# One decode step of a hybrid trunk on one core: dense panels in quarters across nine decode turns, attention pieces first on PE

## What is computed

```python
def mixer_inputs(h, w_in, b_f, w_g2, b_g):
    z = h @ w_in                    # 2048 -> 6168: FoX q, k, v; GLA q, k, v, r; two narrow gate groups
    ...
def fox_sample(q, k_new, v_new, logf_new, k_past, v_past, logf_past):   # decode: 8 requests, 8 heads
    s_past = jnp.einsum('bthd,bshd->bhts', q, k_past, preferred_element_type=jnp.float32) * scale
    ...
    p = jax.nn.softmax(jnp.concatenate([s_past, s_new], axis=-1), axis=-1).astype(v_new.dtype)
    return (jnp.einsum('bhts,bshd->bthd', p[..., :P], v_past)
            + jnp.einsum('bhts,bshd->bthd', p[..., P:], v_new))
def gla_prompt(q, k, v, g): ...     # 4 GLA heads over 256 tokens, in chunks of 64
def gla_chunk(S0, q, k, v, g): ...  # also one step for each decode request's own state
def memory_kv(mem, g_mem, w_k, w_v): ...   # 256 memory tokens
# x += [FoX heads, GLA heads] @ w_out ; x += cross_attn(...) ; x += swiglu(...) ; final rmsnorm
```

## Time and profile before

| | us |
|---|---|
| runs of the kernel | 1799.93, 1797.80, 1799.86 (median 1799.86) |
| the profiled execution | 1794.59 |
| its span, first to last instruction | 1792.9 |
| start to the eighth panel's end | 82.4 |
| turns 0 to 8 and the norm of the heads | 704.6 (82.4 to 787) |
| `out` panels to the end | 1005.9 |

### The profile page before, as it was taken

One profiled execution on the slowest core, in us unless ns is written; L12 is line 12 of the kernel. 1 busy time (PEld: TensorE's weight loads), 2 busy tenths in 40 slices (PEclk: granted clock), 3 DMA queues, 4 the chain that ended last, 5 costly groups with the idle time before them and its releaser, 6 DMA issues.

```text
span 1792.9 us, 33586 instructions
## 1 busy us (share of the span) xinstructions
PE 1571.9 (88%) x12269; PEld 1449.2 (81%) x12269; DVE 1057.7 (59%) x3260; ACT 633.0 (35%) x758; POOL 232.2 (13%) x332
## 2 busy tenths in 40 slices
PE   5999989784965667869967999999999999999997
PEld 5999868673843444569946999999999999999997
DVE  4557868577686886476664555555344555554444
ACT  3342322213242231344344433333333333333443
POOL 3000122222112222213211100000000000000221
PEclk9999989886977757789978999999999999999998
DMA  7456889987869688564541454454455555544553
GB/s 285 174 177 254 334 348 357 374 338 276 309 203 333 224 273 313 195 260 172 181 130 59 142 188 177 176 186 165 148 182 200 182 179 186 184 172 141 181 177 129
DMA packets 85736, 388.24 MB, mean 217 GB/s; under 512 B 9080, under 2 KB 19072, under 8 KB 63760
## 3 DMA queue, kind: packets, MB, share of 16 engines
q1 hardware_dynamic: 36048, 230.90, 36.2%
q0 software_dynamic: 39376, 143.15, 22.0%
q10 hardware_dynamic: 10224, 13.12, 2.1%
HBM read 377.03 MB, written 10.10 MB: 216 GB/s over the span
## 4 chain that ended last, share of the span: by engine, by line
PE 64%; DVE 13%; DMA 4%; issue 3%; ACT 2%; POOLq 0%; POOL 0%; DVEq 0%; ACTq 0%
PE bank L1443 19%; PE bank L1444 18%; PE bank L1445 18%; DVE page L958 4%; DVE wlo L881 2%; DMA page<-vc_dram 2%; PE bank L1562 2%; DMA page<-kc_dram 1%; ACT whi L503 1%; PE bank L1653 1%; DMA g_s<-s_dram 1%; DVE g_dd L1124 0%; DVE g_d L1162 0%; DVE g_s L1132 0%; PE bank L1760 0%
## 5 line engine op out<-in xcount | busy, mean ns | idle before, releaser
L1443 PE MATMUL bank<-hh,whi 128*128 128x264 f32 (+1 forms) x2560 | 739.0, 289 | 13.2 <-DVE wlo L881 8.7
L1444 PE MATMUL bank<-hl,whi 128*128 128x264 f32 (+1 forms) x2560 | 731.0, 286 | 0.0
L1445 PE MATMUL bank<-hh,wlo 128*128 128x264 f32 (+1 forms) x2560 | 730.3, 285 | 0.0
L503 ACT ACTIVATE whi<-raw 128x2048 fp32r<-128x2048 f32 (+1 forms) x232 | 410.2, 1768 | 815.4 <-PE bank L1445 810.4
L881 DVE TENSOR_TENSOR wlo<-raw,whi 128x2048 fp32r<-128x2048 f32 (+1 forms) x232 | 489.1, 2108 | 333.0 <-ACT whi L503 332.7
L1443 PEld LDWEIGHTS bank<-hh,whi 128*128 128x128 f32 x2560 | 488.9, 191 | 25.8 <-issue 20.0
L1444 PEld LDWEIGHTS bank<-hl,whi 128*128 128x128 f32 x2560 | 489.2, 191 | 1.0 <-issue 0.7
L1445 PEld LDWEIGHTS bank<-hh,wlo 128*128 128x128 f32 x2560 | 486.4, 190 | 0.0
L958 DVE CUSTOM_DVE_ANT_0 page<-page,qb 128x128 f32<-128x128 f32 x1024 | 225.4, 287 | 67.6 <-DMA page<-kc_dram 50.1
L1443 PE MATMUL bank<-f_hi,whi 128*128 128x264 f32 x704 | 201.9, 287 | 7.5 <-DVE f_lo L1415 7.5
L1445 PE MATMUL bank<-f_hi,wlo 128*128 128x264 f32 x704 | 201.4, 286 | 0.0
(11 more groups left out here) (273 smaller groups left out, 1266.7 us busy)
## 6 DMA issues: line engine op xcount, KB each, us to landing
raw<-p_gu_dram SPq DMA_DIRECT2D x88, 1024.0 KB, 4.8
page<-kc_dram POOLq DMA_DIRECT2D x128, 512.0 KB, 5.8
page<-vc_dram POOLq DMA_DIRECT2D x128, 512.0 KB, 5.9
raw<-p_dn_dram SPq DMA_DIRECT2D x64, 704.0 KB, 4.0
raw<-p_fox_dram SPq DMA_DIRECT2D x24, 1024.0 KB, 5.0
raw<-p_gla_dram SPq DMA_DIRECT2D x24, 1024.0 KB, 7.1
raw<-p_out_dram SPq DMA_DIRECT2D x16, 1024.0 KB, 4.8
raw<-p_mem_dram SPq DMA_DIRECT2D x8, 1024.0 KB, 8.1
```

The lines of the kernel that those rows point to most:

```text
L503: act.activation(whi[:, kk % 2, 0:blocks * P], raw[:, kk, 0:blocks * P], ACT.Copy).then_inc(S("w_hi"), 1)
L1443: mm(out, blk(whi, k % 2, b), rh, start=start, stop=False)
L1444: mm(out, blk(whi, k % 2, b), rl, start=False, stop=False)
L1445: return mm(out, blk(wlo, k, b), rh, start=False, stop=stop)
```

## The change

The FoX and GLA panels become one list of 48 (`p_in`), with columns in a new order: FoX q, GLA q, k, v, then FoX k and v by head, then GLA r. Eight panels run at the start. The other 40 and the 8 memory panels are cut into quarters of four blocks (12 matmuls) and are dealt over nine turns of 16 parts by the table `QUARTERS`: 8, 8, 3, 3, 5, 5, 6, 4 and 6 panels. A part of a turn has one K page on DVE. In every part PE first does its attention pieces and then the part's quarters. Two more tables deal the V pages (`VALUES`) and the heads (`HEAD_AT`). States are in turns 2 and 3, the GLA heads in turns 2 to 5, the FoX heads in turns 6 and 7, the memory's norm in turn 7, the norm of the GLA heads in turn 8. Head buffers move out of the ring to free parts of `z` and elsewhere; copies of q and v for the heads go, since q is scaled when it leaves the bank and PE reads `z`. The new token's share of the softmax is worked once for all requests in turn 8. POOL fetches the pages in the order in which the parts use them (`page_places`). At the start, panel 0 goes ahead of the sums of the norm, and its weights are loaded after a quarter of x. The `out` panels read their rows from `zr`. All loops over turns are written out. From the `out` panels on the order is as before.

```diff
-MIX = [("k", j) for j in range(8)] + [x for j in range(8) for x in (("v", 2 * j), ("v", 2 * j + 1), ("k", 8 + j))]
+IN, TURNS = 48, 9
+QUARTERS = ([2] * 16,) * 2 + ([1, 1, 1, 0] * 4,) * 2 + ([1, 1, 1, 2] * 4,) * 2 + (
+    [2, 1] * 8, [2] * 4 + [0] * 6 + [1, 1, 1, 1, 2, 2], [2, 1] * 8)
+VALUES = ([0] * 4 + [1, 1, 2] * 4,) * 8 + ([0] * 4 + [2] * 8 + [0] * 4,)
+HEAD_AT = (1, 3, 7, 9, 13, 18, 19, 24)
+def quarters(t, j):
+    first = 32 + sum(sum(q) for q in QUARTERS[:t]) + sum(QUARTERS[t][:j])
+    return [(n // 4, n % 4) for n in range(first, first + QUARTERS[t][j])]
...
+def page_places():
+    where = {}
+    for t in range(TURNS):
+        for j in range(16):
+            if t < ND:
+                where["k", t, j] = len(where)
+            for v in values(t, j) if t else ():
+                where["v", t - 1, v] = len(where)
...
+            first_x(0)
+            weights(0)
+            first_x(1)
+            first_x(2)
...
+            def panel_step(p):
+                act.wait_ge(S("mm_done"), p + 1)
+                panel_cast(p + 2)
...
+            for g in range(16 * TURNS):
+                t, j = g // 16, g % 16
...
+                for p in finished(g - 1):
+                    panel_evac(p)
...
+                elif t < ND:
+                    k_page(t, j)
+                for p in finished(g - 1):
+                    panel_split(p + 2)
...
+                if t >= 1:
+                    softmax_turn(t, j)
...
+            def quarter(p, q):
+                n = T if p < IN else MEM
+                if q == 0:
+                    pe.wait_ge(S("w_split"), p + 1)
+                    pe.wait_ge(S(f"acc{p % 2}_free"), p // 2 + 1)
+                for b in range(4 * q, 4 * q + 4):
...
+                    last = three(bank[p % 2][:, 0:n], p % 4, b, hh[:, b, 0:n], hl[:, b, 0:n], b == 0, b == C - 1)
+                if q == 3:
+                    last.then_inc(S("mm_done"), 1)
...
+            for g in range(16 * TURNS):
+                t, j = g // 16, g % 16
+                if t == 0:
+                    first_turn(j)
+                else:
+                    softmax_turn(t, j)
+                if t in (2, 3):
+                    state_turn(4 * (t - 2) + j // 4, j % 4)
+                if 2 <= t < 6:
+                    gla_turn(t - 2, j)
+                for h in range(H):
+                    head_turn(h, g - 96 - HEAD_AT[h])
...
+                for p, q in quarters(t, j):
+                    quarter(p, q)
+            for c in range(C):
+                out_panel(c)
```

More of the change, by code:

```diff
@@ L419, in square_sums @@
+            for t in range(TURNS):
+                for j in range(16):
+                    if t < ND:
+                        fetch("k", t, j)
+                    for v in values(t, j) if t else ():
+                        fetch("v", t - 1, v)
+            for b in range(8):
+                fetch("xk", 0, b)
             def square_sums(m, go, value):
@@ L557, in q_copy @@
             def q_copy(t):
                 act.wait_ge(S("q_ps"), t + 1)
-                if not (isinstance(t, int) and t == 0):
+                if t:
                     act.wait_ge(S("k_used"), 16 * t)
                 for n in range(2):
-                    ins = act.activation(qb[:, 512 * n:512 * n + 512], bank[2 + n][:, :], ACT.Copy, scale=SCALE)
+                    ins = act.activation(qb[:, 512 * n:512 * n + 512], bank[2 + n][:, :], ACT.Copy)
                 ins.then_inc(S("q_b"), 1)
-            some(1, 2)
@@ L754, in _ @@
-            cast(ST["out"][0], 0, 0, C)
-            cast(ST["out"][0], 0, 1, C)
-            for h in range(GH):
-                act.wait_ge(S("hn_out"), h + 1)
-                act.activation(hh[:, 8 + 2 * h:10 + 2 * h, :], z[:, 32 + 2 * h:34 + 2 * h, :], ACT.Copy).then_inc(S("hn_hi"), 1)
             for c in range(C):
@@ L1059, in _ @@
-            LINKS = 8
-            panel_turn(1, to_z(24), "gla", 0)
-            first = ch.count
-            with dve.Fori(2, 4) as t:
-                ch.turn(first, t - 2, LINKS)
-                panel_turn(t, to_z(24), "gla", 2 * t - 2)
-            ch.after(first, 2, LINKS)
-            dve.wait_ge(S("q_b"), 5)
-            for g in range(4):
-                for c in range(4 * g, 4 * g + 4):
-                    norm_lo(1, c, 2, mem_raw(g)[:, c % 4, :], hh, hl, MEM)
-                (sm_diag, sm_sub, sm_sum, sm_rec)[g](4)
@@ L1561, in pv @@
                     for g in range(4):
[L1562 to L1563 removed]
+                        last = mm(bank[4][32 * g:32 * g + 32, 0:256], prob[:, v, :], page[:, slot, 256 * g:256 * g + 256],
+                                  start=v == 0, stop=v == PAGES - 1)
                     last.then_inc(S("v_used"), 1)
@@ new lines, in _ @@
+            for g in range(16 * TURNS):
+                t, j = g // 16, g % 16
+                if t == 0:
+                    first_turn(j)
+                else:
+                    softmax_turn(t, j)
+                if t in (2, 3):
+                    state_turn(4 * (t - 2) + j // 4, j % 4)
+                if 2 <= t < 6:
+                    gla_turn(t - 2, j)
+                for h in range(H):
+                    head_turn(h, g - 96 - HEAD_AT[h])
+                if t == 7:
+                    memory_turn(j)
+                if t == 8:
+                    last_turn(j)
+                if t <= 6 and j == 15:
+                    if t in (2, 3):
+                        pe.wait_ge(S("gd_out"), 4 * (t - 1))
+                    if t == 6:
+                        pe.wait_ge(S("a_olo"), 4)
+                    q_spread(t + 1)
+                for p, q in quarters(t, j):
+                    quarter(p, q)
```

1606 lines of the change are left out of this document (791 added, 815 removed).

## The result

| | before | after |
|---|---|---|
| median, lowest to highest (us) | 1799.89, 1797.8 to 1800.75 | 1743.72, 1741.5 to 1745.78 |
| profiled span (us) | 1792.9 | 1744.1 |

The ratio is 0.9689, 95% interval 0.9673 to 0.9706: faster by 3.1%. The forecast was 1669 with a range of 1630 to 1735, so the direction was right and the size was not: 75 us are missing.

A forecast was written before the change was run, and what follows sets the result against it. DMA was taken as the limit in one third, chains of small DVE, PE and ACT steps in another. Start 77.4, turns 576 (524 times 1.10) and end 1009, with span and median corrections, gave 1669 us, range 1630 to 1735.

The forecast's parts named there:

- loss factor of 1.10: Turns 0 to 8: lockstep of parts stretches the 524 us floor 1.10 times to 576 us; range 1.02 to 1.23.
- three places that still stall: In the turns: state's read, GLA exponentials, query copy at a GLA turn's end; about 8 us a turn in turns 2 and 3.
- Rival 3: Lockstep where DVE waits for attention results behind PE's quarters: 4.98 us a part, not 4.0; 1810 us; chance 0.07.
- DVE's work: Turns 0 to 8: DVE busy 508 us in sum, beside 502.5 before; hardly removed, only packed.
- PE's work: Turns 0 to 8: 56, 57, 51, 51, 49, 49, 63, 45 and 44 us, a panel taking 5.8, a V page 0.47.
- The floor: Turns 0 to 8: the fullest of DVE, PE and DMA in each turn, 524 us together.
- Rival 1: Page transfers sustain only 354 GB/s over the turns: 1686 us; chance 0.17.
- 410 GB/s: DMA rate assumed for turns 1 to 7, from stretches at 410 and 417 with DVE and PE both short of data.
- Rival 2: PE's clock falls to 0.72 in the turns, as in the earlier head turns: 1733 us; chance 0.13.
- The start: Before turn 0: no wait for constants before the first copy, panel 0 ahead of the sums; 5 us earlier, at 77.4.
- The end: From the `out` panels on: 1005.9 us as before plus 3 for a half-done first panel, 1009 us.
- term of 5.3 us: Added to the sum because the median before lay 5.3 us above the profiled execution, 1799.86 against 1794.59.

The follow-up runs named there:

- E15: The changed kernel with a panel's four quarters run together, in the part that held the last of them: 1817.6 us.
- best version: The changed kernel with quarters first on PE, bank read and split at the end of DVE's part, and the norm's sums ahead of panel 0: 1667.4 us.
- three levers: Work left out of the version with quarters first and late bank read (1675.7 us): 92 us of PE, 1653.2; 109 us of DVE, 1661.8; 65 MB of pages, 1646.5.
- E12: The version with quarters first on PE and bank read and split late in DVE's part (1675.7 us), these two steps one part later: 1689.0 us.

## Why the forecast was wrong, step by step

**The loss factor of 1.10, that is where 71 of the 75 us are.** The forecast stage was 576 us, it took 647. The step that failed is the sentence that nearly every value passes to the next engine one part before it is used, "which is what PE's attention-first order is for", and the list of three places that still stall. In the changed kernel these three places cost DVE 3.0, 1.6 and 6.2 us (the state's read, the exponentials, the query's copy). The list left out the finished panel's bank, 109.7 us. PE's last quarter is the last thing in PE's part, the bank's read the first in DVE's next part: no slack at all, and what stands ahead of the quarter are pieces that themselves wait for DVE. The order rows shown ahead of the forecast held it. By the runs this costs 55 us through the order, 36 to 43 through the slack, and 68 through both.

**Rival 3 came nearest, but by another value.** It had DVE waiting behind the quarters in PE's in-order queue, for an attention result, with idle time before copies from banks 2, 5, 6 and 7 as its sign. That sign is absent: DVE stands 5.5 us in all for PE's small results in these turns. What it waited for was the finished panel itself, in banks 0 and 1. I priced rival 3 for all 144 parts (4.98 us a part), judged that it would not occur in all, and gave it 0.07, with nothing of it in the likeliest case; the wait that came stood in 34 places. With whole panels, in 40 places of 4.9 us, this wait did make the kernel slower than before: from the first diagonal to the first `out` product E15 took 717 us. That this is rival 3's number is chance, since its waits are longer, fewer and for another value:

```profile
82.60:799.70 717.10, 569.11 (x4085) 453.69 (x4086) 488.91 (x2542) 192.12 (x259) 136.61 (x256) 0.86 0.77 277
```

**DVE's work:** forecast 508 us, measured 489. Turn by turn (59, 53, 63, 63, 56, 56, 62, 59, 37 against 51.6, 57.5, 63.3, 60.4, 52.9, 54.6, 55.7, 54.6, 41.7) right within 8 us. "DVE 88% busy" was wrong for the changed kernel (76%) and near for the best version:

```profile
77.60:649.00 571.40, 520.89 (x4080) 423.66 (x4079) 488.52 (x2542) 190.84 (x259) 136.59 (x256) 0.96 0.91 346
```

**PE's work was too small in the sum:** 465 us forecast, 551 measured. I had put it together from prices at full clock and in long rows. The panels' and the V pages' share (82.76 to 732 us, only PE's instructions that read `whi`, and then `page`):

```profile
82.76:732.00 649.24, 321.79 (x1549) 0.90 0.84 307
...
82.76:732.00 649.24, 84.33 (x1024) 0.90 0.84 307
```

322 against 48 x 5.8 = 278, and 84 against 60. Two things are in it. The prices were from start to start in long rows, while busy time also holds the end of each short one: a matmul's record here lasts 0.28 us where the next begins after 0.12, so 192 quarters that stand alone add some 31 us (an estimate, 0.16 each), and a V page alone takes 0.64 us and not 0.47. And some quarters run in part at the 1.2 GHz level (0.22 us a matmul at 398.00 in the changed kernel's chain, after PE had stood 1.13 us, and 0.12 at 401.87). In the best version it is still 521. The total of before, 556 us, was the better guide. It was not what cost most of the time: taking 92 us of PE's work away gave 23, and the best version keeps 521 us of PE in a stage of 571.

**The floor and the factor by what was measured.** Sum of the fullest engine of each turn: 561 us in the changed kernel, which took 655 by these windows, 1.17 times. In the best version, whose windows are not quite turns, the fullest engines make 532 us and the windows 579, 1.09 times. In the changed kernel, then, both terms were above the forecast's, the floor by 37 us and the factor by 0.07, and a floor read from PE's busy time already holds some of what waiting costs. So 524 and 1.10 fit a kernel without the mutual wait. That its 1667.4 comes so near 1669 is partly luck, since PE's size was wrong below it.

**Rival 1 (354 GB/s):** not the cause. Halving the pages gave 21 us, and the best version moves 381 GB/s over 70 us. The Trainium skill's limit of about 358 GB/s for a core ("DMA: Bandwidth & Descriptors", section Specifications) is not borne out here, with one core running. But the forecast's 410 GB/s was not reached over a turn either: those 381 came with a DMA share of 0.99. And one reading behind the 410 was wrong: of the two stretches in which DVE and PE were said to be short of data, PE was busy 9.97 of 10 us in the second. Once the waits are gone, pages give the largest gain of the three levers (29 us).

**Rival 2 (the clock):** not at 0.72. In turns 2 to 5 it was 0.85 to 0.90, and it rises to 0.96 over the stage when the waits go, with PE's instructions unchanged in number. I read it as an effect of the waits more than their cause.

**The start:** forecast 77.4, came at 82.8. With the sums first turn 0 starts at 76.8, so the rest of the step was right (ScalarE's first copy of x starts at 6.15 instead of 10.99), and the panel's half had the wrong sign: I counted what PE could begin sooner and not that the sums, which had lain in a wait, moved onto the path.

**The end:** 1009 us forecast from the first `out` product, 1014 measured (1744.1 - 729.8). About 4 us of this lie in the cross attention (from the last `out` bank to the first `xo` bank 89.6 us, before 85.3). I did not follow it. Against it, the term of 5.3 us from the profiled execution to the median was no constant: here the median lies 2.1 us below (1743.7 against 1744.1 + 1.7).

## What to carry to other kernels

When two in-order engines work through the same numbered parts, write down for every value that crosses, also for the bank of a finished accumulation, the place in the giver's part and in the taker's part: a value given last and taken first has no slack, and if one also crosses the other way, the two engines take turns. Put first in a part what depends on nothing recent (here dense quarters), whatever its urgency, and last what waits; then try one part more and one less, since too much slack starves the next step. If levers on three resources all give the same small gain, stop looking for the fullest engine and look for the loop.

## What the hardware showed that I had not expected

At the start DVE's first split took 2.29 us in some kernels and up to 7.41 in others, for the same instruction. It depends on whether POOL's squares had begun (best version, then the kernel with sums first alone):

```profile
9.78 5.76 POOL L429 TENSOR_TENSOR x_sqs<-x_res 128x1056 f32<-128x1056 f32 x3
...
10.58 7.12 DVE L975 TENSOR_TENSOR wlo<-raw,whi 128x2048 fp32r<-128x2048 f32 x1 [2.21 <-ACT whi L578]
```

```profile
10.80 2.29 DVE L975 TENSOR_TENSOR wlo<-raw,whi 128x2048 fp32r<-128x2048 f32 x1 [2.43 <-ACT whi L578]
...
11.86 7.22 POOL L429 TENSOR_TENSOR x_sqs<-x_res 128x1056 f32<-128x1056 f32 x3
```

In the first, the split ends 2.16 us after POOL's third square (17.70 against 15.54); in the changed kernel again 2.16 us after POOL's second (16.02 against 13.86), its record lasting 5.25. In E12 it ended 2.16 us after POOL's first (14.43 against 12.27). It looks as if the whole split waited for the end of a square, of the first, the second or the third, and then ran at its usual length; in the second kernel DVE began first, and POOL's three squares took 7.22 us instead of 5.76. The Trainium skill says this of two-input VectorE instructions and GpSimd, "SBUF — State Buffer", section "SBUF: two separate sides": the port pair that they share is locked for a whole instruction. The records agree with it, and they show that one wait can last over several of POOL's instructions: in the best version from DVE's start at 10.58 to the end of the third square. No run here changed this alone, so what it costs the kernel stays open.
